# Rescheduling the operand splits of a two-block fp32 transformer kernel: a table of turns in the state-space scan, own banks for keys and values, finer modulation groups

## The reference

```python
# first block
proj = h @ w_in                                   # q, six key/value parts, gates, u, v
h = h + rms_norm(mix @ w_out, g); h = h + rms_norm(swiglu(rms_norm(h, g2)) @ w_down, g3)
# second block
mod = (silu(c) @ ada_w + ada_b)                   # 1024 x 6144
proj = h @ w_in                                   # q_lat, kv_lat, k_idx, w_idx, z, xbc, dt, g_a, g_b
iscore = where(admissible, einsum('bqh,bqhs->bqs', w_idx, rel), -inf); idx = top_k(iscore)
xbc = silu(causal_conv(xbc)); dt = softplus(dt_raw + dt_bias)
y = ssd(x, dt, B, C) + d_skip * x                 # 32 heads of 64, 8 groups, state 128
y_b = rmsnorm(y * silu(z), ssd_norm) @ w_o_ssd    # 2048 x 1024
mix = (sigmoid(g_a) * y_a + sigmoid(g_b) * y_b) @ w_out
```

## Time and profile before

| | |
|---|---|
| median of 3 runs | 972.31 us (971.44 to 973.08) |
| profiled execution, its own time | 969.64 us |
| span of its profile | 967.9 us |
| PE busy | 941.1 us, 97% |
| DVE busy | 663.4 us, 69% |
| ACT busy | 539.5 us, 56% |
| POOL busy | 235.7 us, 24% |
| TensorE clock granted | 1.00 in the stretches read here |

### The profile page before, as it was taken

One profiled execution on the slowest core, in us unless ns is written; L12 is line 12 of the kernel. 1 busy time (PEld: TensorE's weight loads), 2 busy tenths in 40 slices (PEclk: granted clock), 3 DMA queues, 4 the chain that ended last, 5 costly groups with the idle time before them and its releaser, 6 DMA issues.

```text
span 967.9 us, 15371 instructions
## 1 busy us (share of the span) xinstructions
PE 941.1 (97%) x5665; PEld 801.0 (83%) x5665; DVE 663.4 (69%) x1094; ACT 539.5 (56%) x952; POOL 235.7 (24%) x235
## 2 busy tenths in 40 slices
PE   8999999999999999999999999999999999999997
PEld 8987778888877898999878899976678878888786
DVE  5765677777785668965578666677866767755453
ACT  6667575444534668744455466566764654544443
POOL 5304102111122240399932144320200021000100
PEclk9999999999999999999999999999999999999999
DMA  9755357799887813750139666642254777656562
GB/s 287 237 149 178 107 153 256 231 282 279 279 279 238 254 45 118 209 153 22 46 124 340 189 182 188 171 136 66 87 179 149 252 236 236 209 178 193 194 216 69
DMA packets 131352, 179.00 MB, mean 185 GB/s; under 512 B 8124, under 2 KB 96910, under 8 KB 131280
## 3 DMA queue, kind: packets, MB, share of 16 engines
q1 hardware_dynamic: 120384, 144.53, 47.8%
q0 software_dynamic: 10304, 33.18, 11.3%
q10 hardware_dynamic: 592, 0.34, 0.1%
HBM read 176.90 MB, written 1.12 MB: 184 GB/s over the span
## 4 chain that ended last, share of the span: by engine, by line
PE 84%; DVE 7%; ACT 4%; DMA 2%; issue 2%; DVEq 0%; SPq 0%; ACTq 0%
PE bank L1942 17%; PE bank L2022 16%; PE bank L2024 16%; PE bank L2023 16%; DVE w_lo L1333 2%; PE bank L2195 1%; PE bank L2458 1%; DMA w_raw<-in_w_in 1%; PE bank L1973 1%; PE bank L2454 1%; PE bank L2481 1%; DMA w_raw<-in_w_down 1%; ACT w_hi L868 1%; PE bank L2389 1%; PE bank L2077 1%
## 5 line engine op out<-in xcount | busy, mean ns | idle before, releaser
L1333 DVE TENSOR_TENSOR w_lo<-w_raw,w_hi 128x1024 fp32r<-128x1024 f32 (+1 forms) x239 | 282.7, 1206 | 86.9 <-ACT w_hi L868 86.4
L868 ACT ACTIVATE w_hi<-w_raw 128x1024 fp32r<-128x1024 f32 (+1 forms) x266 | 270.4, 1038 | 117.0 <-PE bank L2024 71.1
L2022 PE MATMUL bank<-w_hi,h_hi 128*128 128x512 f32 x448 | 179.2, 400 | 3.4 <-DVE w_lo L1333 3.4
L2024 PE MATMUL bank<-w_hi,h_lo 128*128 128x512 f32 x448 | 174.8, 390 | 0.0
L2023 PE MATMUL bank<-w_lo,h_hi 128*128 128x512 f32 x448 | 174.4, 389 | 0.0
L1942 PE MATMUL bank<-h_hi,w_hi 128*128 128x256 f32 x432 | 124.4, 288 | 2.1 <-DVE h_lo L1486 1.1
L1942 PE MATMUL bank<-h_lo,w_hi 128*128 128x256 f32 x432 | 122.1, 283 | 0.0
L1942 PE MATMUL bank<-h_hi,w_lo 128*128 128x256 f32 x432 | 122.1, 283 | 0.0
L2022 PE MATMUL bank<-w_hi,ff_hi 128*128 128x512 f32 x272 | 107.8, 396 | 3.4 <-DVE w_lo L1333 2.2
L2023 PE MATMUL bank<-w_lo,ff_hi 128*128 128x512 f32 x272 | 106.0, 390 | 0.0
L2024 PE MATMUL bank<-w_hi,ff_lo 128*128 128x512 f32 x272 | 105.9, 389 | 0.0
(11 more groups left out here) (461 smaller groups left out, 1595.9 us busy)
## 6 DMA issues: line engine op xcount, KB each, us to landing
w_raw<-in_w_in SPq DMA_DIRECT2D x84, 512.0 KB, 3.8
ada_raw<-in_ada_w POOLq DMA_DIRECT2D x48, 512.0 KB, 6.3
w_raw<-in_w_gate_up SPq DMA_DIRECT2D x88, 256.0 KB, 5.3
w_raw<-in_w_ffn_in SPq DMA_DIRECT2D x88, 256.0 KB, 4.0
w_raw<-in_w_down SPq DMA_DIRECT2D x22, 512.0 KB, 6.5
w_raw<-in_w_ffn_out SPq DMA_DIRECT2D x22, 512.0 KB, 4.6
w_raw<-in_w_out SPq DMA_DIRECT2D x16, 512.0 KB, 3.6
w_raw<-in_w_o_ssd SPq DMA_DIRECT2D x16, 512.0 KB, 3.6
```

The lines of the kernel that those rows point to most:

```text
L868: act.activation(high(u, n), w_raw[:, u % RING, 0:n], ACT.Copy).then_inc(hi_ready, 1)
L1333: return dve.tensor_tensor(dst, src, hi.bitcast(F32), ALU.subtract)
L2022: pe.matmul(out, x_hi[:, k, x], hi, start=start, stop=False, skip_group_check=True)
L2024: return pe.matmul(out, x_lo[:, k, x], hi, start=False, stop=stop, skip_group_check=True)
```

## The change

Four edits of order and of banks; no instruction is added or removed apart from waits.

1. `kv_blocks` takes banks 2 and 3 in place of the two that the stream would give, and waits for `bias_ready` (long since given) in place of `free_bank`. The first use of a bank after it waits one read earlier.
2. During the down product the modulation goes in groups of two k with one split before each, in place of groups of four with two splits.
3. One split, `split_to(s_z.u0 + 2)`, which makes the low half of z unit 1, stands ahead of the `shut` add; those of units 2 and 3 stay behind it.
4. In the scan a table gives the turns in which a unit is split; G+2 is split ahead of the scan; the g_b steps end two heads earlier (four in place of three for the first two heads), their reads stand one turn earlier, and two steps of `s_os` stand in turn 14.

```diff
-    GB_STEPS = [3 if h < 2 else 0 if h == 12 or h > 28 else 1 for h in range(2 * KI)]
-    GB_READ = (5, 14)
-    OS_STEPS = {KI - 1: 2, KI: 4, KI + 1: 4}
+    GB_STEPS = [4 if h < 2 else 0 if h == 10 or h > 26 else 1 for h in range(2 * KI)]
+    GB_READ = (4, 13)
+    OS_STEPS = {KI - 2: 2, KI - 1: 2, KI: 4, KI + 1: 4}
+    SCAN_UNITS = {0: 4, 3: 5, 4: 6, 7: 7, 8: 8, 10: 9, 11: 10, 13: 11, 14: 12, 17: 13, 18: 14}
@@ ACT, keys and values (and the same on PE, in kv_blocks)
-        k_bank, v_bank = bank3[(s_in.b0 + 2) % 2], bank3[(s_in.b0 + 3) % 2]
+        k_bank, v_bank = bank3[2], bank3[3]
@@ ACT, blocks of xbc
+            if b == s_xbc.n:
+                split_to(s_gb.u0 + 3)
@@ ACT and DVE, scan
-            if i % 2 == 0:
-                split_to(s_gb.u0 + i // 2 + 1 + AHEAD)
+            if i in SCAN_UNITS:
+                split_to(s_gb.u0 + SCAN_UNITS[i])
@@ DVE, down product
-        for h in range(2 * (MOD_FIRST - 5)):
-            split_to(s_dn.u0 + AHEAD + 2 * h + 1)
-            modulate(5 + h // 2, 4 * (h % 2), 4 * (h % 2) + 4)
+        for h in range(4 * (MOD_FIRST - 5)):
+            split_to(s_dn.u0 + AHEAD + h + 1)
+            modulate(5 + h // 4, 2 * (h % 4), 2 * (h % 4) + 2)
@@ DVE, scores
+        split_to(s_z.u0 + 2)
         link(dve.tensor_tensor(isc[:, :, :], isc[:, :, :], shut[:, :, :], ALU.add))
         split_to(s_z.u0 + 4)
@@ PE, kv_blocks
-            free_bank(st, n)
-            free_bank(st, n + 1)
-            k_bank, v_bank = bank3[(st.b0 + n) % 2], bank3[(st.b0 + n + 1) % 2]
+            pe.wait_ge(bias_ready, 1)
+            k_bank, v_bank = bank3[2], bank3[3]
@@ PE, first use behind it
-                    pe.wait_ge(act_read, s_in.act0 + 3)
+                    pe.wait_ge(act_read, s_in.act0 + 2)
```

## The result

| | before | changed |
|---|---|---|
| median | 972.12 us (971.44 to 973.08, 4 runs) | 961.12 us (960.81 to 961.78, 4 runs) |
| profiled execution | 969.64 us | 960.92 us |
| span | 967.9 us | 959.2 us |

The ratio is 0.9887, 95% interval 0.9870 to 0.9904: 11.0 us faster. The forecast was 965.3, 7.0 faster, with a range of 963.6 to 968.6: the right way, and too small. Between the two profiled executions the gain is 8.7 us. So there are two errors to find, 1.7 us in the sum that was made against the trace, and 2.3 us that no term stood for. The first alone would have given 972.31 - 8.7 = 963.6, the edge of the range; the second carries the time out of it. The profiled execution of the changed kernel is one of its four timed ones; that of the kernel before is none of its four.

A forecast was written before the change was run, and what follows sets the result against it. The prediction took PE, busy 97% of the span, as the bound. Gains of 0.9 + 0.2 + 0.8 + 5.1 = 7.0 us from the median 972.31 gave 965.3, range 963.6 to 968.6.

The forecast's parts named there:

- Keys and values: At the keys and values, free banks 2 and 3 remove PE's wait for ACT's read: 0.9 us gained, bounds 0 and 0.9.
- Modulation: In the down product, 1.1 us from the first wait mostly returns at a later load: 0.2 gained, bounds 0 and 1.1.
- z: At the second z unit, a low half ahead of the `shut` add removes PE's wait: 0.8 us gained, bounds 0.6 and 0.9.
- POOL's wait: At z unit 4, PE would want POOL's low half 0.1 to 0.15 us too early.
- Scan: In the scan, six removed waits give 6.3 us, new waits take 1.2: 5.1 gained, bounds 2.6 and 6.3.
- The new waits: In turns 5 and 14 of the scan, PE waits for ACT's reads behind a split: 0.6 us each, 1.2 together.
- I take the same difference from the median: Whole kernel: the profiled execution's 2.67 us below the median was assumed to hold after the change.
- B: Rival: DVE becomes the bound of the scan, 2.4 us come back, total gain 4.5, time 967.8; chance 0.14.
- C: Rival: the first three places' gains return to the next late thing, above all a transfer; 967.0 us; chance 0.12.
- D: Rival: slower, 974.3 us or more, as ACT's scan splits wait for landings or buffers and delay exponents; chance 0.04.
- E: Rival: less than 1.9 us gained, because splits end where PE needs them only by chance; chance 0.04.

The follow-up runs named there:

- the kernel before again: The kernel before with no edit, run and profiled once more: 970.51 us against 970.62, ratio 1.0001.
- the modulation alone: The kernel before with only the modulation in groups of two, one split before each: 969.43 us, ratio 0.9985.
- z alone: The kernel before with only one low half of z moved ahead of the `shut` add: 970.11 us against 971.25, ratio 0.9989.
- only the first group divided: The kernel before with only the first of the modulation's groups cut in two, later groups still in fours: 970.11 us, ratio 0.9986.
- the third set: Later runs on one chip, with the changed kernel unedited beside the kernel before: 961.77 us against 971.12, ratio 0.9916.
- the kernel without them: The changed kernel with G+4, G+5 and O+2 split one turn earlier, so no split precedes ACT's g_b reads: 960.07 us, ratio to before 0.9889.
- the scan alone: The kernel before with only the scan's part (table of turns, g_b steps and reads, G+2 split ahead): 963.85 us, ratio 0.9927.
- the kernel without that wait alone: The kernel before with only the split of the scan's turn 2 moved to turn 1: 967.69 us against 971.25, ratio 0.9966.
- the kernel with late splits: The changed kernel with as many scan splits, each for a unit that PE wants in the next turn: 965.78 us against 961.77.

## Why the prediction was right or wrong

**Keys and values** (0.9): right. The trace gains 0.96 at the place and the times 0.8.

**Modulation** (0.2): wrong. The step that failed is "A unit that PE asks for 1.1 earlier and that lands at the same time makes a wait of 1.1 more there". With the first wait PE gains 1.24 us, and by 304 nothing of it has come back, because the units don't land at the same time. In fours, DVE makes two low halves together and then none for 3.2 us, and SP issues the loads in the same rhythm, two and two; in twos a load goes out every 2.6 us. Two units matter, the fourth and the fifth for whose landing ACT waits. Their high halves in the kernel before, in the kernel before again and with the modulation alone, three profiles in which PE comes to the down product at the same time within 0.1 us:

```profile
297.90 1.06 ACT L868 ACTIVATE w_hi<-w_raw 128x1024 fp32r<-128x1024 f32 x1 [3.82 <-DMA w_raw<-in_w_down]
301.14 1.06 ACT L868 ACTIVATE w_hi<-w_raw 128x1024 fp32r<-128x1024 f32 x1 [2.18 <-DMA w_raw<-in_w_down]
```

```profile
297.83 1.06 ACT L868 ACTIVATE w_hi<-w_raw 128x1024 fp32r<-128x1024 f32 x1 [5.34 <-DMA w_raw<-in_w_down]
299.89 1.06 ACT L868 ACTIVATE w_hi<-w_raw 128x1024 fp32r<-128x1024 f32 x1 [1.00 <-DMA w_raw<-in_w_down]
```

```profile
294.15 1.06 ACT L868 ACTIVATE w_hi<-w_raw 128x1024 fp32r<-128x1024 f32 x1 [1.60 <-DMA w_raw<-in_w_down]
299.30 1.06 ACT L868 ACTIVATE w_hi<-w_raw 128x1024 fp32r<-128x1024 f32 x1 [4.09 <-DMA w_raw<-in_w_down]
```

The fourth decides. Its load goes out at 287.19 in place of 289.11, and it is there 3.7 earlier with the DMA engines as full as before. In both profiles of the kernel before its low half is done just in time for PE, at 300.2; with the modulation alone it is done at 297.2, 1.6 before PE asks. Over all profiles the high half begins at 297.10 to 297.92 in the six with the modulation in fours, and at 292.37 to 294.22 in the six in twos, where PE itself is up to 1.6 ahead. The prediction's mechanism itself is true as long as the modulation is in fours: in the profile of z alone PE happened to come 0.67 earlier, and it waits 0.62 at this very unit.

```profile
300.31 0.50 PE L2023 MATMUL bank<-w_hi,ff_hi 128*128 128x512 f32 x1 [0.62 <-DVE w_lo L1333]
```

The fifth unit is the one of the wait of 0.18 at 303.33, in which the prediction saw the end of the full DMA. It moves by 1.8 or by 0.6, by the profile of before that one takes; the kernel before again doesn't wait for it at all. So 1.2 of the 1.8 are the edit's, which is also what the times say (1.2, with an interval of 0.5 to 2.4); in the comparison of the first profiles the other 0.6 are luck. With only the first group divided, the loads of the two units still go out as a pair and the fourth is there at 297.17, 0.7 earlier. So one earlier load isn't enough for the fourth unit; for the fifth, there at 298.79, it seems to be.

I had said myself that the loads go out "a little earlier in twos" and let the DMA share decide. The rule of the Trainium skill, "DMA: Bandwidth & Descriptors", section "Issuing engines are not separate DMA queues", that transfers of all engines run on the same 16 DMA engines is not contradicted (their share in 282 to 302 is 0.97 in the changed kernel, where it was 0.96), but it doesn't tell which transfer is first, and the gain of 0 that I had drawn from it did not come. The mechanism isn't dead in twos either: in the third set the changed kernel, which comes to the place 0.9 us earlier than in its first profile, had a wait of 0.52 for the fifth unit at 300.32 us.

**z** (0.8): right, 0.7 in the trace; POOL's wait didn't come.

**Scan** (5.1): right in mechanism, a size off by 0.5. The new waits came where they were forecast, in turns 5 and 14. They are shown with 0.34 and 0.43 and cost 0.55 and 0.64, as the starts of the kernel without them tell: 1.19 together, the sum's 1.2. So the term that was too small is that of the removed waits, 6.3, with "I add 0.16 to each wait that goes wholly": 5.6 + 1.2 = 6.8 came back, 0.25 beyond the shown idle time for each of the six. Wait by wait the starts give 0.21 for the one of 1.85, 0.22 for one of 0.78, and 0.27 to 0.29 where a wait stands in an even row of steps (0.95 and 0.66 in the down product). There the second matmul behind the wait starts 0.34 after the first and not 0.23; where a step stands behind an exponent product it is 0.34 for 0.31 or 0.32 without a wait. Theory 2 of the scan alone, 0.27 for every wait, comes to the right total, but it is too high for most of them. The rest, about 0.2 us, is not put down to a place.

The units' leads were told one turn too long in two cases: G+5 is wanted in turn 6, not 7, and G+7 in turn 10, not 11. Both came in time.

**What no term stood for.** "I take the same difference from the median" is the second step that failed. The profiled execution was one that had kept its clock; by their times the four timed ones were not. The wait of 1.85 costs 2.1 us always and 1.5 more when the clock falls behind it, by the mean clocks in about half of the 73 executions (42 at most). Shown by: three profiles in which it fell, all at that place (in windows of 4 us no other stretch ahead of the last 16 us of any trace has less than 0.97); the kernel without that wait alone, which is 3.6 faster and scatters 1.1 us; and the kernel with late splits, which got a wait of 1.57 and the dip with it. Of the 11.0, 8.7 are in the two traces. That 1.5 to 1.7 of the other 2.3 are this loss, with four timed runs that happened to have it, is argued from their times, since those runs have no clock on record; the last 0.6 or so stay open. Whatever they are, they belong to those four runs and not to the change: the median of before is 970.62, 971.25 and 971.12 in the three later sets and 972.12 in the first, and with ten runs of before in one set the difference is 9.35.

**The rivals.** B (DVE the bound) is out: DVE had 35.3 us of work in these turns, not 37.2, and 8.0 us of idle time before its mixing matrices. Only seven of the eight low halves fall into PE's turns 3 to 14, and the multiplications at old L1831 met a fold of POOL's in two turns instead of four and took 6.2 us, not 8.1. Two of the splits met one in their place and took 1.95 and 1.66 for 1.22 (at 667.19 and 681.18), less than the 1.3 more that the prediction allowed. C would have needed returns of the first three gains; none came, beyond 0.2 that belongs to single executions. D and E are out by the result.

## What to carry to other kernels

A wait of the bound engine has three prices: the idle time shown, two or three tenths of a us to get going again, and, if it is long, what the clock takes after it; remove the longest first, and look at several executions' mean clock before a median is compared with one profile. When work is interleaved with a stream's conversion, an even rhythm can bring the loads forward also when the DMA engines are full: follow the issue times before a later wait is counted back, and look whether that wait is there in a second execution of the same kernel. A hand-written order is judged by how many turns a product lies ahead of its use, not by how much work a turn holds.

## What the runs showed of the hardware

* After PE had been idle 1.85 us, or 1.57, in the middle of dense work, the granted clock was 0.50 to 0.70 in the windows of the next 4 us in four of the traces and 1.00 in three others with the same wait of 1.85; it cost 1.5 us each time. None of these traces has such a dip behind the waits of 1.31 (at 116 to 118 us) or of 0.78. What decides between the two outcomes behind the same wait stays open. The Trainium skill, "TensorE: Matmul & The Clock Gate", section "Part 1: The HAM clock gate", says that the clock is set by how busy PE has been recently; the windows with the dip agree, and that the same wait has the effect in some executions of one program and not in others is what these runs add.
* A wait costs PE more than its shown idle time: 0.16 to 0.19 us up to the first start, and before the second matmul 0.11 more in an even row of 128x512 matmuls, but 0.02 to 0.03 behind an exponent product.
* With the DMA engines 0.96 busy, issuing the weight loads one each 2.6 us and not in pairs had one of them there at 294.15 and not at 297.90 (issue 287.19 and 289.11). Between two executions of one kernel the next load differed by 1.25 us (301.14 and 299.89), and a wait of 0.18 came and went with it.
* A low half on DVE that overlapped POOL's fold of 1.29 us took 1.95 us in place of 1.22.
